# Moving the turning of the first half of x1 into the attention loop, and joining attention and mixing in one block

## The reference

```python
x1  = layernorm(sqrt(2) * x  + gla_mixer(x))      # gated linear attention, 4 heads, chunks of 64 rows
out = layernorm(sqrt(2) * x1 + pool_mixer(x1))    # causal pooling of windows 2, 4, 8, 16, a linear map per group, a SiLU gate
```

## Time and profile before

| | |
|---|---|
| median of 3 runs | 1974.26 us (1969.22 to 1974.47) |
| the profiled execution, its own time | 1964.6 us |
| span in its profile | 1962.9 us |
| mean granted TensorE clock | 0.981 of full |
| PE busy | 1861.6 us (95%) |
| DVE busy | 1398.3 us (71%) |
| ACT busy | 852.5 us (43%) |
| POOL busy | 598.2 us (30%) |
| DMA | 336.43 MB, 171 GB/s mean |

### The profile page before, as it was taken

The page is one execution under the profiler, slowest core; times in us unless marked ns, Lnnn a source line. Parts: engine busy times, 40 slices in busy tenths (PEclk is TensorE's granted clock), DMA queues, the critical chain, the costliest instruction groups (busy, mean ns, idle before and its releaser), DMA issues.

```text
span 1962.9 us, 24653 instructions
## 1 busy us (share of the span) xinstructions
PE 1861.6 (95%) x8688; PEld 1535.0 (78%) x8688; DVE 1398.3 (71%) x1769; ACT 852.5 (43%) x1323; POOL 598.2 (30%) x380
## 2 busy tenths in 40 slices
PE   8989999999999699999679999999999998999997
PEld 7878887886788588888558888887888786887786
DVE  3454555778667678787666788768899967546997
ACT  4554445657555434333444444344333344224221
POOL 1322231332221000000145665405566532323330
PEclk9999999999999799999879999999999999999999
DMA  8967572557365645443413544242546326556442
GB/s 286 321 200 266 195 248 97 152 141 247 90 171 179 239 145 188 171 162 138 171 43 116 170 150 144 98 172 75 178 170 221 140 93 215 208 192 257 161 151 97
DMA packets 259725, 336.43 MB, mean 171 GB/s; under 512 B 18208, under 2 KB 187936, under 8 KB 255904
## 3 DMA queue, kind: packets, MB, share of 16 engines
q1 hardware_dynamic: 259616, 335.02, 50.9%
HBM read 218.58 MB, written 116.39 MB: 171 GB/s over the span
## 4 chain that ended last, share of the span: by engine, by line
PE 38%; DVE 7%; issue 4%; ACT 1%; POOL 0%; DVEq 0%; ACTq 0%; POOLq 0%
PE banks L200 13%; PE banks L202 12%; PE banks L201 12%; DVE m_w_lo L2520 2%; DVE m_x_lo L2534 1%; DVE m_win_a L2550 1%; ACT m_x_hi L2310 0%; DVE m_res L2633 0%; DVE m_win_b L2550 0%; DVE m_x_lo L2512 0%; PE banks L2203 0%; PE banks L2250 0%; DVE m_win_b L2566 0%; DVE m_res L2617 0%; DVE m_x_lo L2494 0%
## 5 line engine op out<-in xcount | busy, mean ns | idle before, releaser
L200 PE MATMUL banks<-m_x_hi,m_w_hi 128*128 128x512 f32 x1320 | 517.7, 392 | 12.6 <-DVE m_z L2596 6.6
L201 PE MATMUL banks<-m_x_lo,m_w_hi 128*128 128x512 f32 x1320 | 515.1, 390 | 0.0
L202 PE MATMUL banks<-m_x_hi,m_w_lo 128*128 128x512 f32 x1320 | 514.9, 390 | 0.0
L200 PEld LDWEIGHTS banks<-m_x_hi,m_w_hi 128*128 128x128 f32 x1320 | 248.8, 188 | 68.7 <-DVE m_w_lo L2520 10.6
L202 PEld LDWEIGHTS banks<-m_x_hi,m_w_lo 128*128 128x128 f32 x1320 | 248.7, 188 | 52.1
L201 PEld LDWEIGHTS banks<-m_x_lo,m_w_hi 128*128 128x128 f32 x1320 | 248.6, 188 | 51.8 <-issue 0.7
L200 PE MATMUL banks<-b_hi,h_w_hi 128*128 128x512 f32 x656 | 257.9, 393 | 6.1 <-issue 4.5
L202 PE MATMUL banks<-b_hi,h_w_lo 128*128 128x512 f32 x656 | 256.3, 391 | 0.0
L201 PE MATMUL banks<-b_lo,h_w_hi 128*128 128x512 f32 x656 | 256.0, 390 | 0.0
L2298 ACT ACTIVATE m_w_hi<-m_s 128x512 fp32r<-128x512 f32 x184 | 115.5, 629 | 186.2 <-PE banks L202 166.0
L2436 POOL TENSOR_TENSOR m_s<-pair_raw 128x512 f32<-128x512 f32 x24 | 46.7, 1945 | 469.0 <-POOLq L1512 365.1
(11 more groups left out here) (276 smaller groups left out, 3363.2 us busy)
## 6 DMA issues: line engine op xcount, KB each, us to landing
b_raw<-x_in SPq DMA_DIRECT2D x14, 1024.0 KB, 9.8
p_in<-in_pool_w_in SPq DMA_DIRECT2D x32, 256.0 KB, 5.7
w_fused<-p_out SPq DMA_DIRECT2D x32, 256.0 KB, 3.5
x_in<-h_terms SPq DMA_DIRECT2D x8, 1024.0 KB, 4.3
v_tiles<-h_v_out SPq DMA_DIRECT2D x16, 512.0 KB, 4.0
in_raw<-in_gla_w_in SPq DMA_DIRECT2D x16, 512.0 KB, 5.3
h_raw<-in_gla_w_in SPq DMA_DIRECT2D x16, 512.0 KB, 5.9
k<-k_tiles SPq DMA_DIRECT2D x32, 256.0 KB, 4.2
```

The costliest lines, as they stand in the source:

```text
L200: nc.tensor.matmul(out, a_hi, b_hi, start=first, stop=False, skip_group_check=True)
L201: nc.tensor.matmul(out, a_hi, b_lo, start=False, stop=False, skip_group_check=True)
L202: return nc.tensor.matmul(out, a_lo, b_hi, start=False, stop=last, skip_group_check=True)
```

## The change

1. **Epoch 0 is turned during attention.** In steps t = 8 to 15 (c = t - 8 = 0 to 7) of the attention loop, chunk c takes a quarter of the columns (2 x 256) of two tiles of x1, c // 2 and c // 2 + 4, one after the other through one SBUF buffer `stage_rows`. Per chunk: two loads of 256 KB, two times four transposes into `sum_ps` (the bank of the mean), two copies on ACT, four sums on POOL, seven stores into `x_terms[0]`. The hardware loop ends at t = 7, and the steps from 8 on are written out.
2. **Attention and mixing share one block.** No barrier stands between them. The functions now return pieces of code which `gla_pool_trunk` chains on each engine. PE enters `product(0, 0)` after waits for the banks (`banks_read`). The last residual, shift, scale and norm of attention are interleaved with the first turns of mixing on DVE and ACT. `load_first` loads the weights and the first three terms once all of chunk 7 is stored; the other four are loaded after the last y; term number 5 of the order (j = 3) after `store_last`.
3. **Epoch 0 is handled like the later ones**: `turn_hi`, `turn_lo` on whole 128x2048 terms; `LAST_OF_EPOCH` begins with -1, and with that products 4 and 5 of step 0 are native. `turn_first`, `first_parts`, `first_terms`, `first_sums`, `first_terms_lo` and the POOL parts are gone. SBUF is laid out anew.
4. **At the start of attention** the last four stores of g, half of the loads of the output weights and the load of the norm's weights come after the barrier instead of before it.

```diff
@@ attend_and_norm
+    stage_rows = p.place("a_stage_rows", [P, 2, 2 * P])
...
-        with engine.Fori((TAIL + 1) // 2, NT // 2 - 1) as pair:
+        with engine.Fori((TAIL + 1) // 2, STAGED // 2) as pair:
             for s in range(2):
                 step(pair * 2 + s, s, TAIL, pair)
-        for t in range(NT - 2, NT + TAIL):
-            step(t, t % 2, TAIL, t // 2)
+        for t in range(STAGED, end):
+            step(t, t % 2, TAIL, t // 2, t - STAGED)
...
+        def load_stage_rows(c, pair, kk, r):
+            if r:
+                sp.wait_ge(st_turned, c * 2 + 1)
+            else:
+                if c:
+                    sp.wait_ge(st_turned, c * 2)
+                sp.wait_ge(out_stored[kk], (pair - 1) * DMA)
+                sp.wait_ge(out_stored[1 - kk], (pair + (kk - 2)) * DMA)
+            rows = p.x1[ds((pair + 4 * r - STAGED // 2) * P, P), :].rearrange("p (h c) -> p h c", h=2)
+            sp.dma_start(stage_rows[:], rows[:, :, kk * 2 * P:(kk + 1) * 2 * P]).then_inc(st_rows, DMA)
+
+        def store_stage(c, pair, kk):
+
+            sp.wait_ge(st_sum, c * 4)
...
+                sp.dma_start(p.x_terms[0, j - 1, :, k:k + 2, cols], src).then_inc(st_stored, DMA)
...
+        def step(t, s, lag, pair, c=None):
                 static = isinstance(t, int)
+            if staged(c):
+                load_stage_rows(c, pair, s, 0)
                 if lag >= 1 and not (static and t + 1 >= NT):
                     sp.wait_ge(gated_done, t)
                     load_g(t + 1, 1 - s)
                 if has(t, lag, TAIL):
                     sp.wait_ge(out_done, (t - TAIL) * 2 + 2)
                     sp.dma_start(p.x1[ds((t - TAIL) * P, P), :], out[1 - s][:]).then_inc(out_stored[1 - s], DMA)
-                if lag >= LAG and not (static and t >= NT):
-                    sp.wait_ge(y_read, (t - LAG) * 2 + 2)
-                    load_x(t, s)
+            if staged_before(c):
+                store_stage(c, pair, s)
                 if not (static and t + 2 >= NT):
                     sp.wait_ge(o_mm, t + 1)
                     p.load_qkv(sp, t + 2, s)
+            if staged(c):
+                load_stage_rows(c, pair, s, 1)
+            if lag >= LAG and not (static and t >= NT):
+                sp.wait_ge(y_read, (t - LAG) * 2 + 2)
+                load_x(t, s)
+            if static and t == NT:
...
+                sp.wait_ge(st_stored, CHUNKS * PRODUCTS * DMA)
+                load_first(sp)
...
+        def mean(t, c):
 
                 pe.wait_ge(sum_lo_done, t)
                 pe.wait_ge(rms_mid, t - 1)
+            if staged_before(c):
+                pe.wait_ge(st_copied, c * 2)
...
+        def turn_stage(t, c, r):
+
+            pe.wait_ge(st_rows, (c * 2 + (r + 1)) * DMA)
+            if r:
+                pe.wait_ge(st_copied, c * 2 + 1)
+            else:
+                pe.wait_ge(rms_mid, t)
+            for b in range(4):
+                last = nc.tensor.transpose(sum_ps[:, b * P:(b + 1) * P], stage_rows[:, b // 2, b % 2 * P:(b % 2 + 1) * P],
+                                           p.ident[:])
+            last.then_inc(st_turned, 1)
...
                     outputs(s)
+            if staged(c):
+                turn_stage(t, c, 0)
                 if has(t, lag, LAG):
-                    y_half(t, s, 1, lag)
+                y_half(t, s, 1, lag, c)
+            if staged(c):
+                turn_stage(t, c, 1)
...
+        def copy_stage(c, r):
+
+            act.wait_ge(st_turned, c * 2 + (r + 1))
+            if c:
+                act.wait_ge(st_sum, c * 4)
+                act.wait_ge(st_stored, c * (PRODUCTS * DMA))
+            stage = stage_b if r else stage_a
+            nc.scalar.activation(stage[:].rearrange("p h k t -> p (h k t)"), sum_ps, ACT.Copy).then_inc(st_copied, 1)
@@ pool_mix_and_out
+    def load_first(sp):
+        p.load_pair(sp, p.pair_raw0, TILES[0], 0)
+        for n, dst in enumerate((ahead[0], ahead[1], first_raw)):
+            sp.dma_start(dst[:], p.x_terms[0, ORDER[n] - 1]).then_inc(x_loaded[n], DMA)
...
+        y_ended()
+        load_x(0, 3)
             load_pair(1)
+        load_x(0, 4)
+        load_x(0, 6)
+        store_last()
+        load_x(0, 5)
...
-            for n in range(HT):
-                turn_first(n)
+        banks_read()
```

More of the change, by code:

```diff
@@ L49 @@
 class Program:
-    ROWS, ROWS_PREFETCHED = 4, 4
+    ROWS = 2
     QKV_LOADS = 5
@@ L1864, in pool_mix_and_out @@
     rstd = [p.place(f"m_rstd{b}", [P, 1]) for b in range(2)]
+    assert p.at <= p.scores_at
+    p.at = p.scores_at
+    raw = [p.pair_raw0, p.place("m_pair_raw1", [P, 2 * KT, P])]
+    for j in (1, 5, 4):
+        place_w(j)
+    assert p.at <= p.kn_at
+    p.at = p.kn_at
+    for j in (1, 5):
+        place_hi(j)
+        place_lo(j)
+    carry = p.place("m_carry", [P, MT, PAD])
+    assert p.at <= p.qkv0_end
+    p.at = p.qkv0_end
+    place_hi(4)
+    place_lo(4)
+    assert p.at <= p.state_at
+    s1, s2, s3, s4 = (p.place(f"m_s{n}", [P, HALF_K, P]) for n in range(1, 5))
+    place_w(6)
     shared_at = p.at
@@ L1931, in turns_to, with loaded @@
     def turns_to(e, n):
-        return PRODUCTS * (e - 1) + TURNS.index(n) + 1
+        return PRODUCTS * e + TURNS.index(n) + 1
+    def loaded(e, n):
+        if n < PRELOADED:
+            return ahead[n][:]
+        return first_raw[:] if (e, n) == (0, 2) else x_raw[ORDER[n]][:]
     def turning(turned, i, slot):
-        return [(epoch(i - later) + 1, n) for n, (later, at) in turned.items() if at == slot and follows(i - later)]
+        return [(LAST_OF_EPOCH.index(i - later), n) for n, (later, at) in turned.items()
+                if at == slot and i - later > 0 and follows(i - later)]
     def epoch(i):
-        return sum(i > last for last in LAST_OF_EPOCH)
+        return sum(i > last for last in LAST_OF_EPOCH) - 1
     def group(i):
@@ new lines, in tensor, with turn_stage, free, operands @@
+    def tensor(pe, banks_read, y_banks_read):
+        def turn_stage(c):
+            t, kk = c // 2, c % 2
+            for s in range(2):
+                if kk == 0:
+                    pe.wait_ge(rows_loaded[s], (t + 1) * DMA)
+            if c:
+                pe.wait_ge(stage_copied, 2 * c)
+            for s in range(2):
+                for half in range(2):
+                    for k in range(2):
+                        first = (half * HALF_K + 2 * kk + k) * P
+                        last = nc.tensor.transpose(p.ps[:, 6 + s, (half * 2 + k) * P:(half * 2 + k + 1) * P],
+                                                   rows[s][:, first:first + P], p.ident[:])
+            last.then_inc(stage_turned, 1)
+        def free(i, j):
+            o = i - 2
+            if j == 1 and o >= 0:
+                pe.wait_ge(*((c11_copied, o + 1) if o < MIX else added(o, 3)))
+            elif j == 5 and o >= 0:
+                pe.wait_ge(*((c12_added, o + 1) if o < MIX else added(o, 5)))
+            elif j in (6, 2):
+                pe.wait_ge(seeded, i + 1)
+            elif j == 7:
+                pe.wait_ge(*((u2_copied, i + 1) if i < MIX else added(i, 2)))
+            elif j == 3:
+                pe.wait_ge(*((p5_copied, i + 1) if i < MIX else added(i, 1)))
+            elif j == 4:
+                pe.wait_ge(*((u3_added, i + 1) if i < MIX else added(i, 4)))
+        def operands(i, n):
+            s, j, e = set_of(i), ORDER[n], epoch(i)
+            if native(i, n):
+                pe.wait_ge(*weights_ready(s, j))
+                pe.wait_ge(x_loaded[n], (e + 1) * DMA)
+                return
+            pe.wait_ge(w_lo_done, parts_to(s, n))
+            if follows(i - 1) or follows(i - 2):
+                pe.wait_ge(x_lo_done, turns_to(e, n))
+        def product(i, n):
+            j = ORDER[n]
+            operands(i, n)
+            if n == 0 and i < 2:
+                nc.tensor.matmul(bank(i, 6), w_hi[1][:, 0, :], x_hi[1][:, 0, :], start=True, stop=True)
+            free(i, j)
+            opens = j in (1, 5)
+            for k in range(HALF_K):
+                if native(i, n):
+                    last = nc.tensor.matmul(bank(i, j), weights(set_of(i), j)[:, k, :], x_raw[j][:, k, :],
+                                            start=opens and k == 0, stop=k == HALF_K - 1, skip_group_check=True)
+                else:
+                    last = split_product(nc, bank(i, j), w_hi[j][:, k, :], w_lo[j][:, k, :], x_hi[j][:, k, :],
+                                         x_lo[j][:, k, :], opens and k == 0, k == HALF_K - 1)
+            last.then_inc(product_mm, 1)
+        banks_read()
+        for i in range(STEPS):
+            for n in range(PRODUCTS):
+                product(i, n)
+            if i == FIRST_CHUNK:
+                y_banks_read()
+            if 0 <= i - FIRST_CHUNK < CHUNKS:
+                turn_stage(i - FIRST_CHUNK)
```

1835 lines of the change are left out of this document (895 added, 940 removed).

## The result

The changed kernel takes **2016.9 us** (median of 4 runs, 2014.3 to 2019.1) beside 1973.7 for the kernel before on the same chip: ratio 1.0223, 95% interval 1.0202 to 1.0244. It is slower, by 43.2 us where +18.2 was forecast, and above the range of 1970 to 2006.

The account below looks back on a forecast made before the run. The prediction took PE to bound attention, with idle time at the seams. Loop +49.8, passage to mixing -28.6 and start of attention -3 gave +18.2 us on 1974.3, so 1992 us, range 1970 to 2006.

Parts of the forecast that it names:

- The gap: PE idle before a chunk's second turn, its load queued behind twelve SP transfers; 4.7 us, in t = 9 to 13.
- the sum: Loop steps 8 to 15 +49.8, passage to mixing -28.6, start of attention -3: +18.2 us in all.
- the landing, 4.9 us: Second tile's load, from SP's issue to data there, right behind five q, k, v loads; between 3.3 and 5.9 us.
- the clock, 2.1 us a step: PE's clock falls in each gap, so transposes, scores and following chain come 2.1 us later: +8.4 per such step.
- rows 11: Trace of PE's clock before the change: fell some 2 us after the last y, still 0.50 after attention's start.
- The mixing steps [...] are as before: Mixing from step 1 on and the rest of the kernel were to cost nothing extra: 0 us.
- The seam, -28.6: From the last turn of attention to mixing step 1: 58.2 us where it took 86.8.
- The start, -3: Start of attention: four stores leave the barrier's path, but the second tile's q, k, v wait for them; -3 us.
- A: Rival: the clock holds through the loop's gaps; 0 to +12 us, 1982 us, chance 0.2.
- B: Rival: second tile arrives in time, no gap; 1966 us (chance 0.08), or 1951 with the copy in time (0.06).
- C: Rival: landing 5.9 us, slower term loads, no gain at the start; above +32 us, chance 0.06.
- D: Rival: passage to mixing shrinks less, its chain of stores, loads and splits being longer; 3 us either way, no chance given.

Follow-up runs that it names:

- load_order: Changed kernel with the second tile's load moved on SP's queue ahead of the seven stage stores and five q, k, v loads: 1973.1 us, ratio 1.0003.
- stores_moved_only: Changed kernel with only the seven stage stores moved to the head of the next step: 1996.5 us, ratio 1.0134.
- fill_gap: Changed kernel plus 20 matmuls that compute nothing ahead of the second turn of chunks 0 to 5: 2004.0 us, ratio 1.0155.
- layout_only: Kernel before, with only the mixing's tiles placed at the changed kernel's addresses: 1977.3 us, ratio 1.0022.
- early_second_qkv: stores_first with tile 1's q, k, v loads directly behind the four g stores at the start of attention: 1950.1 us, ratio 0.9890.
- own_buffer: Changed kernel with a second buffer and semaphore for the second tile, both loads at the step's head: 1970.5 us, ratio 0.9995.
- stores_first: Changed kernel, one buffer, second load ahead of q, k, v, ACT's copy ahead of norm_scale, stage stores at next step's head: 1953.6 us, ratio 0.9915.

## Why the prediction was right or wrong

- **The gap: right in place and cause.** The load was issued at the mean + 14.0 (measured 14.1), the gaps stand before the second turn, the clock is lowered by them, and the mean stalls in t = 15. load_order shows the cause: 44 us come back when one load is issued twelve transfers earlier. What failed is the size of terms of the sum. By the profiled spans the sum is 31.4 us short, 15.0 of it in the loop, 7.8 in the mixing, 4.2 at the seam, 1.6 at the start and 2.8 before attention.
- **First step that failed: the landing, 4.9 us.** It is 5.6 to 6.5. I placed the load between a lone one and the last of the five, since it is only 256 KB; but behind the five it takes longer than their last (stores_moved_only: 6.1). With it the five gaps of t = 9 to 13 are 29.1 us for the 23.5 of the sum, and t = 14 and 15, which were to have none, have 0.82 and 1.19. The 2.6 us estimated from the Trainium skill (DMA: Bandwidth & Descriptors, Anatomy of one DMA) was further off than my own number for this load; 3.2 to 3.4 us, in load_order, is nearest to it. That section gives its formula for DMAs issued by GpSimd, which the prediction didn't say, and these are SP's.
- **Second step: the clock, 2.1 us a step, too small and in one step missing.** fill_gap has 25.0 us at full clock against 28, so 3. I also let step 9 go free of it since the gap in step 8 would be short; that gap was 3.37 us, and the clock fell after it. My own reading of rows 11, a fall some 2 us into an idle stretch, spoke against leaving it out. At 3 us a step these are about 7.5 us of the loop's 15.0 (3 in t = 9 and 0.9 in each of t = 10 to 14), an estimate from fill_gap; the longer gaps are 5.6, and some 2 us are left.
- **By step:** the second turns are 9.8, 9.9, 10.3, 11.2 and 10.0 us later than before's 18.15 from step to step in t = 9 to 13 (forecast 6.4 and 8.4 four times), +6.1 in 14 (3.7), +2.8 in 15 (3.2), and step 8 +4.7 (2.9, where the sum took a landing of 4.6 and not 4.9). Together 64.8.
- **Third step: "The mixing steps [...] are as before".** The change moves every tile of the mixing, and I priced that at nothing. It measured +7.8 us in the profile and +4.9 by layout_only.
- **The seam, -28.6: nearly right (-24.4).** The first product comes 31.0 us after the last turn (forecast 32.3); what is missing lies in the native products, cold (6.18 us) and 4.4 us late for their load.
- **The start, -3:** -1.4 in the profile. The barrier's wait became one for v, as the prediction said it might; early_second_qkv cuts that wait by 3.7 us.
- **Rivals.** A (the clock holds through the gaps) falls. B is own_buffer, built on purpose: 1966 forecast, 1970.5 measured; with the copy in time 1951, measured 1960.1. Of these misses the layout's 4.9 us is the known part. C (above +32 us, chance 0.06) is what came, with its longer landing; the clock's price and the layout, which did more, C didn't have. D: the seam did shrink 4.2 us less, but not by the chain that D names, which was 1.3 us shorter. With the load in time alone the changed kernel only equals the one before (load_order 1.0003, own_buffer 0.9995); it pays once the copy and the stores have their places too (stores_first 0.9915).

## What to carry to other kernels

When a step is moved into a tuned loop, write its transfers into the queue's order and ask of each what stands ahead of it: here one load behind twelve other transfers cost 44 us, all that the change lost, by the time that SP took to issue them and by a longer landing behind five of them. A second buffer did no more than the right order. A gap at the engine that sets the time costs more than its length if the clock falls, and it hides other waits, so fix the largest first and measure the small ones again. A change of placement is an edit of its own; run it alone.

## What the runs showed of the hardware

- The same 256 KB load landed 3.2 to 3.4 us after its issue when it stood ahead of the five loads on the queue (load_order), 5.5 to 6.5 us when it stood right behind them (steps 8 to 13 of the changed kernel and of stores_moved_only), and 3.2 to 3.6 us right behind seven stores (steps 14 and 15 of the changed kernel). In stores_first, ahead of the five, it took 3.1 to 5.7 us, and why is open.
- PE's clock: it fell to 1.2 GHz for a while after every gap ahead of a second turn of 2.76 to 6.2 us (steps 8 to 13 of the changed kernel and of stores_moved_only). After shorter gaps both were seen: it stayed at 2.4 GHz after six of the seven of 1.6 to 1.7 us in load_order and fell after the one of 1.71; it held after 2.12 us and fell after 1.86 and 2.56 in fill_gap; and of two gaps of 2.61 us ahead of a mean it held after the one in own_buffer and fell after the one in stores_moved_only (0.69 over 968 to 972). The length of the gap alone doesn't decide it here. Twenty matmuls that compute nothing, in each of six gaps, were worth 13 us.
- Products of the same shape ran at 0.70 or 0.68 us for three matmuls, by the addresses of the mixing's tiles alone (layout_only). I know no reason.
